# mLSTM stage: value and output-gate tiles between the heads' steps, values turned by identity products, fewer one-row products

## The chip, the core and the metric

The kernel runs on one core of a Trainium2 chip. The metric is the device time of one execution in microseconds (us); lower is better. TensorE (PE) multiplies, ScalarE (ACT) and VectorE (DVE) work on tiles, SyncE (SP) issues the DMAs that stream the weights.

## The reference

Two blocks of two layers each over x of 512 tokens x 1024 channels, all in float32. The first block is attention with convolution and Fourier branches and gates, for a context of 256 tokens and for x. The second has a convolution/LRU mixer in layer 0 and an mLSTM mixer in layer 1, each followed by a gated feed-forward part. What the change touches:

```
# first block, each layer and stream: the value heads of attention
z = h @ w_in[l];  v = z[..., OFF_V:OFF_G]            # 128 channels: 2 heads x 64
o = einsum('bgrqk,bkgd->bqgrd', softmax(q k^T / 8), v)

# second block, layer 1: mLSTM, 8 heads, q and k 64 wide, v and o 128 wide
u = xn @ w_in + b_in;  q, k, v, o, ig, fg = split(u)
# per head, causal over the sequence, b = cumsum(log_sigmoid(fg))
d_w    = exp(b_j - b_s + ig_s - m_j)
scores = (q k^T / 8) * d_w
h      = scores @ v / max(|sum(scores)|, exp(-m))
h      = h * rsqrt(mean(h*h) + 1e-6) * head_g
h      = sigmoid(o) * h
out    = h @ w_out
```

## The kernel before

**Layout.** Activations lie with channels on partitions and the 512 tokens along the free dimension. A matrix is streamed as tiles of 128 x 1024 numbers (512 KB) through a ring of four buffers. `split` on ACT rounds a tile to `w_hi` (L680), `lower_w` on DVE makes the rest, `w_lo` (L1919); both run three tiles ahead of PE. A float32 product is three PE products, `three` (L1251 to L1253): hi x hi, lo x hi and hi x lo. One tile of 128 output channels is 8 blocks x 3 = 24 products of 512 columns (`product`). An ordinary tile is read by ACT and then `posted` by DVE; PE's `ready` waits for both `w_ready` and `post`.

**Order.** Each engine runs one hand-written program in order; semaphores join them. There is no scheduler.

**mLSTM stage before.** After the norm `pre_mix`, `ml_qk` works 8 q/k tiles and 8 output-gate tiles with sigmoid, `ml_gates` one tile of the input and forget gates, `ml_v` 8 tiles of values in two halves. `ml_v` wants tokens on partitions, so there the activations are the loaded operand and the weights stream, and the bias row is added by one-row products (L1732), two per token block. Then `mlstm` runs head by head. A head has four steps n (128 keys each). `spread` copies the head's two rows over all partitions by two products of 8 rows (L1757, float32). `score_t` (L1772, L1773) makes the transposed scores of a step, DVE adds the causal mask (`diagonal`, L2565), ACT takes exponentials (L871, L873), DVE multiplies (`weights`, L2575), ACT and DVE split the result (`upper_part` L883, `lower_part` L2582), PE multiplies by the values and by ones (`values`, L1251 to L1253 and L1788, L1789). `query_key_parts` of the next head (L865 on ACT, L2554 and L2555 on DVE) stands in step 1. After a head, DVE makes the denominator (L2592, L2593), ACT copies and squares the numerator (L889, L890) and squares the denominator (L897), PE sums the squares in `total` (L1797, and one-row products L1798). At the end `small` gets the roots, PE spreads them (L1828) and DVE does three operations per head (L2619, L2624, L2627), the second of which multiplies by the output gate. No weight tile is worked in `mlstm`.

**Attention before.** At the end of the tiles of a block, `v_tile` on PE makes the values with tokens on partitions: per token block of 128, 8 x 3 products of only 128 columns. `attention` mixes the heads' steps with other weight tiles (`fill`); ACT and DVE split a tile (`split`, `lower_w`) at its last block, k == 7. At its end DVE does `reciprocals(1)` (L2204) and then raises `post` (L2249), for which the next stage `merge` waits on PE.

## Time and profile before

| | us |
|---|---|
| median of 3 runs (3703.87 to 3711.55) | 3707.84 |
| the profiled execution, whole | 3709.84 |
| its span | 3708.1 |
| PE busy in it | 3425.5 (92%) |
| DVE busy | 2104.3 (57%) |
| ACT busy | 1268.1 (34%) |
| mean granted TensorE clock, share of full speed | 0.927 |

The profile holds one execution. "Busy" of PE is modelled from the starts of pipelined products, so a busy PE can still be at half its clock; the granted clock is a column of its own. A wait is put down to the operation that released it.

### The profile page before, as it was taken

Reading aid. Unit: us, or ns where it says so; the run is one execution under the profiler, and the core shown is the slowest. Engines: PE = TensorE matmul, PEld = TensorE weight load, DVE = VectorE, ACT = ScalarE, POOL = GpSimd, SP = SyncE. Lnnn points to the kernel's source line nnn. Section 1 sums busy time; section 2 is a strip of 40 time slices with the busy share of each in tenths; the row PEclk is TensorE's granted clock in tenths of the full one; section 3 lists DMA queues with packets and bytes.
Section 4 is the critical chain, followed back from the end, with each engine's and each line's share of the span. In section 5 each row is a group of like instructions: output and inputs, shape, how many; then the busy total and the mean of one; then the engine's idle time right before and its main releaser. Section 6 shows DMA issues by size and latency. Waiting matters only on the chain.

```text
span 3708.1 us, 45259 instructions
## 1 busy us (share of the span) xinstructions
PE 3425.5 (92%) x16528; PEld 2802.7 (76%) x16528; DVE 2104.3 (57%) x2898; ACT 1268.1 (34%) x1816; POOL 0.2 (0%) x4
## 2 busy tenths in 40 slices
PE   6999999998999999998999999469999898889997
PEld 4888988776778877876878887257888765678886
DVE  7767876664565555655565557764335323453335
ACT  5554443554222223354222223222222324432221
POOL 0000000000000000000000000000000000000000
PEclk8999999999999999999999999679999895589998
DMA  6554542323222222222222222112223220013221
GB/s 216 188 190 148 184 143 86 119 97 102 85 91 96 96 88 89 79 80 80 91 85 96 96 96 68 34 46 84 98 97 103 68 74 6 1 53 101 96 97 68
DMA packets 98583, 353.69 MB, mean 95 GB/s; under 512 B 10641, under 2 KB 11793, under 8 KB 98450
## 3 DMA queue, kind: packets, MB, share of 16 engines
q1 hardware_dynamic: 98160, 350.82, 28.5%
q8 instruction: 89, 1.46, 0.2%
q10 hardware_dynamic: 290, 1.05, 0.1%
q14 instruction: 44, 0.36, 0.0%
HBM read 349.73 MB, written 2.10 MB: 95 GB/s over the span
## 4 chain that ended last, share of the span: by engine, by line
PE 84%; DVE 10%; ACT 3%; issue 1%; DMA 1%; DVEq 0%; ACTq 0%; SPq 0%
PE ring L1251 23%; PE ring L1252 22%; PE ring L1253 22%; PE ring L1500 2%; PE bank L1251 2%; PE bank L1253 2%; PE bank L1252 2%; PE bank L1292 2%; DVE z L2398 1%; DVE w_lo L1919 1%; ACT w_hi L680 1%; DVE scr L1962 1%; DVE h_lo L1968 1%; PE bank L1757 1%; PE ring L1529 1%
## 5 line engine op out<-in xcount | busy, mean ns | idle before, releaser
L1251 PE MATMUL ring<-h_hi,w_hi 128*128 128x512 f32 (+1 forms) x2888 | 1088.6, 377 | 58.8 <-DVE h_lo L1968 30.4
L1919 DVE TENSOR_TENSOR w_lo<-raw,w_hi 128x1024 fp32r<-128x1024 f32 x658 | 803.6, 1225 | 521.8 <-ACT w_hi L680 499.6
L1252 PE MATMUL ring<-h_lo,w_hi 128*128 128x512 f32 (+1 forms) x2888 | 1073.2, 372 | 0.0
L1253 PE MATMUL ring<-h_hi,w_lo 128*128 128x512 f32 (+1 forms) x2888 | 1072.0, 371 | 0.0
L680 ACT ACTIVATE w_hi<-raw 128x1024 fp32r<-128x1024 f32 x658 | 693.1, 1056 | 812.4 <-PE ring L1253 728.1
L1251 PEld LDWEIGHTS ring<-h_hi,w_hi 128*128 128x128 f32 x2888 | 554.5, 192 | 182.4 <-issue 55.6
L1253 PEld LDWEIGHTS ring<-h_hi,w_lo 128*128 128x128 f32 x2888 | 555.6, 192 | 92.3
L1252 PEld LDWEIGHTS ring<-h_lo,w_hi 128*128 128x128 f32 x2888 | 557.0, 193 | 84.4
L1251 PE MATMUL ring<-y_hi,w_hi 128*128 128x512 f32 (+1 forms) x1328 | 488.7, 368 | 33.7 <-DVE y_lo L1935 26.2
L1252 PE MATMUL ring<-y_lo,w_hi 128*128 128x512 f32 (+1 forms) x1328 | 485.7, 366 | 0.0
L1253 PE MATMUL ring<-y_hi,w_lo 128*128 128x512 f32 (+1 forms) x1328 | 485.4, 366 | 0.0
L1251 PEld LDWEIGHTS ring<-y_hi,w_hi 128*128 128x128 f32 x1328 | 251.0, 189 | 82.3 <-DVE y_lo L1935 28.8
L1253 PEld LDWEIGHTS ring<-y_hi,w_lo 128*128 128x128 f32 x1328 | 251.2, 189 | 40.4
L1252 PEld LDWEIGHTS ring<-y_lo,w_hi 128*128 128x128 f32 x1328 | 251.3, 189 | 39.2
L1183 ACT ACTIVATE scr<-ring 128x512 f32<-128x512 f32 (+1 forms) x96 | 50.6, 527 | 295.2 <-PE ring L1253 295.2
L2303 DVE SCALAR_TENSOR_TENSOR x<-ring,mod,x 128x512 f32<-128x512 f32 (+1 forms) x80 | 60.0, 751 | 155.5 <-PE ring L1253 155.5
L2324 DVE TENSOR_TENSOR z<-scr 128x512 f32<-128x512 f32 (+1 forms) x96 | 57.9, 603 | 153.3 <-ACT scr L1183 153.3
L2200 DVE TENSOR_TENSOR y_lo<-z,y_hi 128x512 fp32r<-128x512 f32 (+1 forms) x112 | 72.4, 648 | 74.5 <-ACT y_hi L1103 74.0
L2190 DVE TENSOR_REDUCE mx<-ring 128x1 f32<-128x768 f32 (+1 forms) x80 | 67.9, 849 | 69.8 <-PE ring L1530 69.2
L1103 ACT ACTIVATE y_hi<-bank 128x512 fp32r<-128x512 f32 (+1 forms) x112 | 63.6, 568 | 106.7 <-PE bank L1253 106.3
L1979 DVE TENSOR_TENSOR scr<-scr 128x512 f32<-128x512 f32 (+1 forms) x152 | 93.8, 617 | 5.2
L2506 DVE TENSOR_TENSOR z<-z,ring 128x512 f32<-128x512 f32 x48 | 33.0, 688 | 110.8 <-PE ring L1253 110.8
(286 smaller groups left out, 3340.2 us busy)
## 6 DMA issues: line engine op xcount, KB each, us to landing
raw<-ws SPq DMA_DIRECT2D x658, 512.0 KB, 3.3
x<-x_t SPq DMA_DIRECT2D x1, 2048.0 KB, 14.6
out_t<-x SPq DMA_DIRECT2D x1, 2048.0 KB, 7.3
xc<-ctx_t SPq DMA_DIRECT2D x1, 1024.0 KB, 9.7
z<-ropes ACTq DMA_DIRECT2D x2, 512.0 KB, 3.5
mat<-mats SPq DMA_DIRECT2D x1, 320.0 KB, 4.4
vec<-vecs SPq DMA_DIRECT2D x1, 216.5 KB, 2.6
xc<-bv ACTq DMA_DIRECT2D x1, 4.0 KB
```

What stands on the lines that cost most here:

```text
L680: nc.scalar.activation(w_hi[:, t % R, :], raw[:, t % R, :], ACT.Copy).then_inc(w_hi_ready, 1)
L1103: nc.scalar.activation(y_hi[:, 4 + k % 2, :T], bank[k % 2][:, :T], ACT.Exp, scale=HEAD ** -0.5)\
L1251: nc.tensor.matmul(o, a_hi, b_hi, start=start, stop=False)
L1252: nc.tensor.matmul(o, a_hi, b_lo, start=False, stop=False)
L1253: return nc.tensor.matmul(o, a_lo, b_hi, start=False, stop=stop)
L1292: m = nc.tensor.matmul(bank[tt][:, 0:1], src[:, tt * P:(tt + 1) * P], ones[:, 0:1], start=k == 0, stop=is_summed or k == KB - 1)
L1500: m = nc.tensor.matmul(fl.bank(job)[0:4, 0:256], c_parts[:, n % 2 * 4 + k // 2, :], weights, start=(n % 2, k) == (0, 0), stop=(n % 2, k) = ...
L1919: nc.vector.tensor_tensor(w_lo[:, u, :], raw[:, u, :], f(w_hi[:, u, :]), ALU.subtract).then_inc(w_ready, 1)
L1979: step(nc.vector.tensor_tensor(total, total, scr[:, 3, :T], ALU.add))
L2190: nc.vector.reduce_max(mx[:, h % 2, qt:qt + 1], view[:, 0:n_kt * P], AX_X).then_inc(s_max, 1)
L2200: nc.vector.tensor_tensor(y_lo[:, b, :T], src, f(y_hi[:, b, :T]), ALU.subtract).then_inc(s_p, 1)
L2303: step(nc.vector.scalar_tensor_tensor(o, ring[:, c % R, :T], g, o, ALU.mult, ALU.add), post)
```

## The change

In the mLSTM stage the gate tile comes first, then 9 tiles (8 of q/k and the values of head 0). The other 7 value tiles and the 8 output-gate tiles become `fill` inside `mlstm`: 16 block products a head, 6, 2, 4 and 4 of them in steps 0 to 3 (head 7: one tile). A value tile is now made with channels on partitions, gets its bias by ACT, and is turned to tokens on partitions by four float32 products with the identity (`v_turned`). The bias comes by 8 new loads on SP at the kernel's start instead of one on ACT. Output gates are Tanh with a half of the bias instead of Sigmoid, and DVE multiplies the numerator by 1 + tanh when it takes it from PSUM; the factor two goes into the root (scale 4/P). The denominator's square is added on DVE into one row of the squares, so `total` has 4 products where it had 8. The row spread for the denominator and the products by ones have 32 output rows instead of 128. In the first block `v_tile` becomes an ordinary tile and `v_turned`, `split` and `lower_w` of a fill tile stand at its first block, and `post` is raised ahead of the last reciprocal.

```diff
@@ plan, mLSTM @@
-    add("ml_qk", 16)
     add("ml_gates", 1)
-    add("ml_v", 8)
-    add("mlstm", 0)
+    add("ml_qk", 9)
+    add("mlstm", 15)
@@ SP @@
+            for h in range(N_HEADS):
+                sp.dma_start(v_bias[:, h:h + 1], bv_in[0:1, h * P:(h + 1) * P].rearrange("o p -> p o")).then_inc(s_bv, 16)
@@ ACT, mlstm @@
+                def v_upper(h):
+                    act.wait_ge(s_turned, C.next(s_turned))
+                    nc.scalar.activation(v_parts(y_hi, h), turned_bank(h).rearrange("p (t d) -> p t d", d=P), ACT.Copy)\
+                        .then_inc(hi_ready, 1)
+                def fill(h, n):
+                    if h == 7 and n > 1:
+                        return
+                    t = 2 * h + n // 2
+                    c = first + t
+                    if n % 2 == 0:
+                        split(c)
+                        return
+                    done(c)
+                    if t % 2 or h == 7:
+                        nc.scalar.activation(z[:, 8 + h, :], fill_bank(h, 1), ACT.Tanh, bias=o_bias[:, h:h + 1],
+                                             scale=0.5).then_inc(s_gate_read, 1)
+                    else:
+                        nc.scalar.activation(z[:, 15, :], fill_bank(h, 0), ACT.Identity, bias=v_bias[:, h + 1:h + 2])\
+                            .then_inc(s_gate_read, 1)
+                    if n == 3:
+                        v_upper(h + 1)
@@ PE, mlstm @@
+                def v_turned(h):
+                    if h:
+                        pe.wait_ge(s_gate_read, gate0 + 2 * h - 1)
+                    for tt in range(4):
+                        s = slice(tt * P, (tt + 1) * P)
+                        m = nc.tensor.matmul(turned_bank(h)[:, s], z[:, 15, s], ident, start=True, stop=True)
+                    m.then_inc(s_turned, 1)
-                    nc.tensor.matmul(ring[:, 3, j], ones_r[:, :], kv[:, b, j], start=n == 0, stop=False)
+                    nc.tensor.matmul(bank[3][0:32, j], ones_r[:, 0:32], kv[:, b, j], start=n == 0, stop=False)
-                        nc.tensor.matmul(o, xv[:, h % 2, t], ones[:, 0:1], start=True, stop=False)
-                        m = nc.tensor.matmul(o, den_sq_row[:, t], ones[HEAD:HEAD + 1, 0:1], start=False, stop=True)
+                        m = nc.tensor.matmul(bank[1][:, 4 * h + tt:4 * h + tt + 1],
+                                             xv[:, h % 2, tt * P:(tt + 1) * P], ones[:, 0:1], start=True, stop=True)
                     for n in range(4):
                         if n < 2:
                             score_t(h, n + 2)
-                        elif h + 1 < N_HEADS:
+                        elif more:
                             score_t(h + 1, n - 2)
+                        if more:
+                            fill(h, (range(6), range(6, 8), range(8, 12), range(12, 16))[n])
+                        elif n < 2:
+                            fill(h, (range(6), range(6, 8))[n])
                         if n == 1 and h:
                             total(h - 1)
+                        if n == 3 and more:
+                            v_turned(h + 1)
                         values(h, n)
@@ DVE, mlstm @@
+                    dve.wait_ge(s_gate_read, gate0 + (2 * h + 2 if h < 7 else 15))
+                    issue(nc.vector.scalar_tensor_tensor(head_out(h), z[:, 8 + h, :], 1.0, ring[:, 2, :],
+                                                         ALU.add, ALU.mult), s_gated)
+                def denominator(h):
+                    step(nc.vector.scalar_tensor_tensor(den_row, den_row, float(P * EPS), den_row, ALU.mult, ALU.mult))
+                    sq = xv[one_row, h % 2, :]
+                    issue(nc.vector.tensor_tensor(sq, sq, den_row, ALU.add), s_den_sq)
-                        issue(nc.vector.tensor_tensor(o, o, z[:, 8 + n - 1, :], ALU.mult), t_ready)
@@ attention, PE @@
-                        m = three(bank[3][:, s], h_hi[:, k, s], h_lo[:, k, s], *w(c, k), k == 0, k == KB - 1)
+                    m = nc.tensor.matmul(bank[3][:, s], z[:, 13, s], ident, start=True, stop=True)
@@ attention, ACT; DVE's lower_w(c) alike @@
+                        if k == 0:
+                            split(c)
                         if k < 7:
                             continue
-                        split(c)
@@ attention, DVE, its end @@
-                reciprocals(1)
                 dve.sem_inc(post, len(fl.tiles))
                 C.next(post, len(fl.tiles))
+                reciprocals(1)
```

PE, step 0 of head 1 in `mlstm`, before, from its values on: L1251 to L1253 are the values' three products, L1788 and L1789 those by ones, L1757 the spread of head 2, L1772 and L1773 the last scores, L1797 and L1798 the total of head 0.

```order
L1251 MATMUL ring<-kv,y_hi 128x512
L1252 MATMUL ring<-kv,y_hi 128x512
L1253 MATMUL ring<-kv,y_lo 128x512
L1788 MATMUL ring<-kv,ones_r 128x512
L1789 MATMUL ring<-kv,ones_r 128x512
L1757 MATMUL bank<-xc,mat 128x512 x2
L1772 MATMUL ring<-kv 128x128
L1773 MATMUL ring<-kv 128x128
L1797 MATMUL bank<-mat,xc 128x1
L1798 MATMUL bank<-mat,xc 128x1
```

The same place now; L1279 to L1281 are the three products, with `h_hi` and `w_hi` those of a fill tile, and `32x512` has 32 output rows.

```order
L1833 MATMUL bank<-kv,ones_r 32x512
L1834 MATMUL bank<-kv,ones_r 32x512
L1799 MATMUL bank<-xc,mat 128x512
L1801 MATMUL bank<-xc,mat 32x512
L1814 MATMUL ring<-kv 128x128
L1815 MATMUL ring<-kv 128x128
L1279 MATMUL bank<-h_hi,w_hi 128x512
L1280 MATMUL bank<-h_lo,w_hi 128x512
L1281 MATMUL bank<-h_hi,w_lo 128x512
```

Two block products of a fill tile (six rows) now stand between the last scores and the total; six blocks, four and four stand in the other steps.

DVE, steps 0 and 1 of a head, before: weights, denominator of the head before (two rows L2592, L2593), diagonal, lower part, then step 1 and the query and key parts of the next head (L2554, L2555).

```order
L2575 TENSOR_TENSOR scr<-ring,scr 128x384
L2592 TENSOR_TENSOR xc<-ring,xc 1x512
L2593 SCALAR_TENSOR_TENSOR xc<-ring,xc 1x512
L2565 TENSOR_TENSOR scr<-xc,mat 128x128
L2582 TENSOR_TENSOR kv<-scr,kv 128x512
L2575 TENSOR_TENSOR scr<-ring,scr 128x256
L2565 TENSOR_TENSOR scr<-xc,mat 128x128
L2582 TENSOR_TENSOR kv<-scr,kv 128x384
L2554 TENSOR_TENSOR kv<-z,kv 64x512
```

Now, from the lower half of the turned values (L2641) on:

```order
L2641 TENSOR_TENSOR y_lo<-ring,y_hi 128x4x128
L2613 TENSOR_TENSOR scr<-ring,scr 128x384
L2627 TENSOR_TENSOR xc<-bank,xc 1x512
L2628 SCALAR_TENSOR_TENSOR xc<-bank,xc 1x512
L2631 SCALAR_TENSOR_TENSOR z<-z,ring 128x512
L2603 TENSOR_TENSOR scr<-xc,mat 128x128
L2620 TENSOR_TENSOR kv<-scr,kv 128x512
L2635 SCALAR_TENSOR_TENSOR xc<-xc 1x512
L2637 TENSOR_TENSOR xc<-xc 1x512
L1967 TENSOR_TENSOR w_lo<-raw,w_hi 128x1024
L2613 TENSOR_TENSOR scr<-ring,scr 128x256
L2603 TENSOR_TENSOR scr<-xc,mat 128x128
```

Ahead of the diagonal of step 2 (L2603) stands the gated numerator (L2631), and ahead of that of step 3 also two row operations and a whole `w_lo`.

DVE, the end of the attention of x in layer 0, before and after; L2204 and L2252 are the same reciprocal, L2178 and L2226 the columns of the modulation:

```order
L2169 TENSOR_TENSOR z<-z,scr 128x512
L1919 TENSOR_TENSOR w_lo<-raw,w_hi 128x1024
L2178 TENSOR_TENSOR mod<-ring,vec 128x4
L2204 RECIPROCAL scr<-scr 128x512
L1919 TENSOR_TENSOR w_lo<-raw,w_hi 128x1024 x2
```

```order
L2219 TENSOR_TENSOR z<-z,scr 128x512
L2226 TENSOR_TENSOR mod<-ring,vec 128x4
L2252 RECIPROCAL scr<-scr 128x512
L1967 TENSOR_TENSOR w_lo<-raw,w_hi 128x1024 x2
L2310 TENSOR_TENSOR z<-z,bank 128x512 x2
```

The last `w_lo` has gone from between the last tile's sum and the reciprocal to ahead of it; the raise of `post`, no row of its own, stood behind the reciprocal and stands ahead of it.

## Rows read from the trace of the kernel before

**Rows 1.** Busy time by stretch: start:end, length, busy us (instructions) PE PEld DVE ACT POOL, granted clock, DMA.
```profile
2800.00:2850.00 50.00, 50.00 (x222) 41.38 (x222) 21.08 (x26) 12.56 (x14) 0.00 (x0) 1.00 0.31 104
...
3100.00:3150.00 50.00, 46.68 (x127) 32.59 (x126) 17.20 (x38) 21.20 (x45) 0.00 (x0) 0.50 0.00 0
```

**Rows 2.** Chain that ended last, in the mLSTM stage: start us, length us, engine and line.
```profile
2998.38 1.05 PE bank L1732 x2
...
3069.77 3.79 PE bank L1757 x4
...
3078.62 0.77 PE ring L1251
...
3097.18 3.70 PE bank L1757 x4
...
3117.36 3.70 PE bank L1757 x4
...
3225.40 0.71 DVE xc L2592
...
3232.05 3.45 PE bank L1828 x16
3235.52 0.75 DVE z L2619
```

**Rows 3.** Instructions grouped by line, 2900 to 3250: busy us, mean ns, idle before.
```profile
L1797 PE MATMUL bank<-mat,xc 128*128 128x1 f32 x64 | 18.6, 359 | 2.3 <-ACT xc L897 2.3
```

**Rows 4.** Instructions in order of time in one head's steps 0 and 1: start, length, engine.
```profile
3112.44 0.70 DVE L2592 TENSOR_TENSOR xc<-ring,xc 1x512 f32<-1x512 f32 x1 [0.64 <-PE ring L1789]
...
3114.22 0.40 ACT L871 ACTIVATE scr<-scr,small 128x128 f32<-128x128 f32 x1 [0.18 <-DVE scr L2565]
...
3117.01 2.58 ACT L865 ACTIVATE kv<-z 64x512 fp32r<-64x512 f32 x4
```

**Rows 5.** PE alone, stretches of 5 us in `ml_v`: busy (instructions), granted clock, DMA share, GB/s.
```profile
3000.00:3005.00 5.00, 5.00 (x17) 1.00 0.00 0
...
3035.00:3040.00 5.00, 5.00 (x9) 0.50 0.00 0
```

**Rows 6.** PE alone, stretches of 2 us in and behind an attention.
```profile
798.00:800.00 2.00, 2.00 (x9) 0.50 0.61 211
...
892.00:894.00 2.00, 1.89 (x5) 0.50 0.00 0
...
896.00:898.00 2.00, 2.00 (x8) 0.79 0.08 31
```

**Rows 7.** PE's waits, context (52:290) and x of layer 0 (540:900): us, times, longest.
```profile
PE ring L1251 <- DVEq L2249: 3.2, 1, 3.2
...
PE ring L1500 <- ACT z L1066: 5.9, 6, 2.4
PE ring L1251 <- DVEq L2249: 5.0, 1, 5.0
```

**Rows 8.** DVE in order of time, end of the attention of x, layer 0.
```profile
887.23 1.23 DVE L1919 TENSOR_TENSOR w_lo<-raw,w_hi 128x1024 fp32r<-128x1024 f32 x1
...
888.56 3.35 DVE L2204 RECIPROCAL scr<-scr 128x512 f32<-128x512 f32 x1
```

**Rows 9.** PE in order of time: first and last of `v_tile`'s 48; then float32 128x128; total-like sums.
```profile
111.75 0.22 PE L1251 MATMUL bank<-w_hi,h_hi 128*128 128x128 f32 x1
...
116.95 0.28 PE L1253 MATMUL bank<-w_hi,h_lo 128*128 128x128 f32 x1
...
101.96 0.45 PE bank L1375 x4
...
2875.48 1.05 PE L1292 MATMUL bank<-mat,scr 128*128 128x1 f32 x8 [2.29 <-DVEq L1982]
```

**Rows 10.** The start: chain of waits; then the DMA queue's packets, MB, share in 8:20.
```profile
7.69 12.23 DMA raw<-ws
...
q1 hardware_dynamic: 2493, 4.65, 104.8%
```

More of the change, by code:

```diff
@@ L969, in v_tile, with v_upper @@
                 done(c)
+                nc.scalar.activation(z[:, 13, :T], bank[2][:, :T], ACT.Copy).then_inc(evac, 1)
+            def v_upper(stream):
+                T = length(stream)
+                act.wait_ge(s_turned, C.next(s_turned))
                 kt = 0 if stream == "main" else SEQ // P
@@ L1569, in attention @@
                     fill(qt)
-                pe.wait_ge(post, first + R)
+                    if qt == 0:
+                        if main:
+                            pe.wait_ge(s_rot_read, C.next(s_rot_read, 5))
+                        v_turned(stream, first + R)
                 max_row(0)
@@ new lines, in fill @@
+                def fill(h, steps):
+                    for s in steps:
+                        t, k = 2 * h + s // 8, s % 8
+                        c, gate = first + t, t % 2 or h == 7
+                        if k == 0:
+                            pe.wait_ge(w_ready, c + 1)
+                            if h == 7:
+                                pe.wait_ge(s_gate_read, gate0 + 14)
+                            elif gate:
+                                pe.wait_ge(s_fill_read, fill0 + h + 1)
+                            elif h:
+                                pe.wait_ge(s_gate_read, gate0 + 2 * h)
+                        m = three(fill_bank(h, t % 2), *w(c, k), h_hi[:, k, :], h_lo[:, k, :], k == 0, k == 7)
+                        if k == 7:
+                            m.then_inc(tile_done, 1)
@@ L1742, in mlstm @@
+                v_turned(0)
                 pe.wait_ge(s_row, C.next(s_row, 2))
@@ L2604, in mlstm @@
                     if n == 0 and h:
-                        denominator(h - 1)
+                        numerator(h - 1)
                     if k + 2 < 4 * N_HEADS:
```

278 lines of the change are left out of this document (135 added, 143 removed).

## Prediction

> **What bounds the kernel now.** I read the busy times by stretch first, then the chain of waits, then single instructions. In a stretch of plain tiles PE is busy all the time at full clock: 222 products of 512 columns in 50 us [rows 1], 0.225 us each, so a tile of 24 costs 5.40 us. In the mLSTM stage PE is again 93% busy, but at a granted clock of 0.50 (1.2 GHz), and no weights are streamed [rows 1]. So the stage is bound by PE at half its clock, and for a smaller part by the handing on between PE, ACT and DVE. One head takes 20.2 us, from one spread to the next (3097.18 to 3117.36) [rows 2]. Two things can be won: a pass of work less, and the clock.
>
> A difference of 0.2% (7 us) is about what a measurement of this kernel can tell from none. All sums stand against the profiled execution, 3709.8 us with a span of 3708.1; the median of the runs is 2 us lower, which I take into the range.
>
> **The mLSTM stage, on PE.** The old stage from the first bias product to the end of the last values runs from 2998.4 to 3225.4 [rows 2]. Seven of the 16 tiles ahead of it have moved into the heads, so the new stage starts 7 x 5.40 = 37.8 us earlier, at 2960.6; old length from there 264.8 us.
>
> New prices at full clock. 512 columns 0.225, 384 in proportion 0.169, 256 about 0.115 and 128 columns 0.111 (48 products from 111.75 to 116.95 [rows 9]): a set of a head's four widths is 0.62 us. A head has two sets for the scores and five for the values and ones, 4.3 us. Fewer output rows change none of this, since the columns stay. The spread is two float32 products: 3.70 us at half clock [rows 2]; at full clock between 1.85 (half) and 2.1 (the one-row product of the same width, 1.05 each [rows 2]); I take 1.95. The total has four products, 8 instructions: 1.05 us [rows 9] where 16 cost some 4.1 at half clock (64 instructions of L1797 begin the same way [rows 3]). Turning the values is four float32 products, 8 instructions at the 0.112 of four in 0.45 [rows 9], 0.9 us. With two tiles, 10.8, a head is 19.0 us on PE. Over the stage: 15 tiles 81.0, scores and values 8 x 4.33 less the two scores ahead of it 34.2, seven times spread, total and turn 27.3; together 142.5 us.
>
> To this come, in order:
> - Start. From the last tile's end to the third score there are ACT's copy, the turn, the columns, the spread, ACT's and DVE's parts of q and k, exponentials and weights. From the spread to the first values the old kernel took 8.9 us (3069.77 to 3078.62 [rows 2]). With 1.0 for copy and post, 0.9 for the turn, 1.3 for the columns, and the last 1.4 of the old chain now under fill, less 2 for a spread at full clock: 8.7 us. PE is half idle there, so 1 us for a start at half clock.
> - The wait for query and key parts. I walk a head from the end of the last values. DVE does the lower half of the turned values, weights, the two row operations (0.71 each [rows 4]) and the gated numerator by 3.4 us and the diagonal by 3.7; ACT's exponentials end at 4.4, its threshold row at 5.0, the split of a tile at 6.1; DVE's `w_lo` (1.23 [rows 8]) at 7.3, weights and diagonal of step 3 at 8.0; ACT's exponential (0.40 [rows 4]) at 8.4, its four parts (2.58 [rows 4]) at 10.9, DVE's two of 0.7 at 12.3. PE reaches the first scores of the next head at 10.7: 4.3 to the values of step 0, then 1.1, 1.95, 0.1, 1.35 of fill, 1.05 and 0.8. It waits 1.6 us. Bounds 0 and 3; seven heads, 11.2 us. At step 0 the same walk has lower part and PE meet at 4.3, no wait. The last head has half a fill: 1.5 us.
> - The clock. Full clock held through alternating one-row and dense products (1.00 at 3000) but, once low, stayed low under the same mix (0.50 at 3035) [rows 5]. Ten dense block products a head will raise it. But spread, total and the wait of 1.6 us stand close together, and in the attention short waits dropped it for some 3 us (0.50 at 798 [rows 6]). I count one such drop in most heads: 1.2 us for each of eight, 10 us. Bounds 0 and 31 (below).
> Sum 8.7 + 1 + 142.5 + 11.2 + 1.5 + 10 = 174.9, against 264.8: **89.9 us gained**.
>
> ACT and DVE carry more, but hide. By the busy times a head of 20.2 us holds 8.6 us of ACT and 6.9 of DVE [rows 1]. ACT gets two splits, two readings and the turned copy and loses two operations; were each of the five as long as `w_lo` (1.23 [rows 8]), it would come to 15. DVE gets two `w_lo`, four operations of 0.7, 12 in all. Both lie under 21 of PE. If that cover goes, the wait above is where it shows.
>
> The end. Before, 23.9 us from the last denominator (3225.40) to `mix_out`; the final loop from 3235.52 [rows 2] had three operations a head on DVE. One goes: 8 x 0.6 less the part that overlaps, 3.8 us. DVE has three more operations ahead of the last total where ACT had one, +1.4; eight instructions fewer in it, -1.5. **3.9 us gained**.
>
> **The value tiles of the first block.** x: 96 products of 128 columns at 0.111 are 10.6 us [rows 9]; now 5.40 and a turn of 0.9, 4.3 gained, twice. Context: 5.3 becomes 2.9 + 0.45, 2.0 gained, twice. PE is the bound there. **12.6 us**, bounds 8 and 13.
>
> **The raise of `post`.** PE waits 5.0 us at `merge` in x of layer 0, and for the same line and as long in layer 1; 3.2 in the context [rows 7]. In those waits lie `w_lo` 1.23, then the reciprocal of 3.35 [rows 8]. Both leave them: `w_lo` to the tile's start, the reciprocal behind `post`. Left is the small column operation, 0.4 us a time, so 12.0 gained. Late next is the reciprocal itself, which PE wants only behind the second tile, over 5 us later. The clock falls to 0.50 behind such a wait and stays low into the stretch at 896 [rows 6]: 5 us at half clock cost 2.2 us of work there, and where it rises sooner 1 or less; 3.7 in all. **15.7 us**, bounds 12 and 16.
>
> **`split` at the tile's start.** PE waits for the reading of a gate 5.9 us in six places in x of layer 0 [rows 7], since ACT does the split (about 1 us, under DVE's 1.23) ahead of it. Up to 1 us a place can go, about as much in layer 1, and some in the context; but the split now stands ahead of exponentials. **6 us gained**, bounds -3 (a loss) and 14.
>
> **The start.** SP issues 8 loads of 128 single numbers behind x and ahead of the first streamed tile, and the chain runs through that tile: 12.23 us of waiting for its DMA, then ACT and DVE [rows 10]. No row shows packets of 4 bytes. 2493 packets, mostly of 1 to 2 KB, took 12 us, 4.8 ns each [rows 10]; the 1024 new ones would take 4.9 us if each costs the same. Bounds 0 (queue not full) and 8. I take a **loss of 5 us**. The Trainium skill, "DMA: Bandwidth & Descriptors", section "Latency and other measured facts", speaks against this edit: a non-contiguous last dimension lowers to one descriptor per element, which is the count of 1024 above. By that page's table a 4 KB load of 64 packets takes 0.68 us, an estimate of 10.9 us for 1024 at the same rate; the sum would be 6 us worse. No row here decides it.
>
> **Sum.** 89.9 + 3.9 + 12.6 + 15.7 + 6 - 5 = 123.1; 3709.8 - 123.1 = 3586.7. **Forecast 3587 us.**
>
> **Rivals.**
> - Full clock and full cover: no drop, and parts in time. For it: the clock held at 3000 [rows 5], and in the attention most short waits didn't drop it. Against: my walk. 10 + 11 less: 3566.
> - Two drops a head, one behind spread and total, one at the wait, each as long as at the start of `merge` (892 into 896 [rows 6], 2.2 us lost): 7 x 2 x 2.2 = 31 instead of 10: 3608. For it: the half clock of the old stage through the same spread [rows 1]. The Trainium skill, "TensorE: Matmul & The Clock Gate", Part 4, says that transposes in PE's transpose mode don't count as busy for the clock; these are plain products with an identity, and it would make this rival likelier if it held for them. The four identity products in 0.45 us [rows 9] ran at full clock.
> - Slower: the fill hides nothing. If PE did the 15 tiles between chains that last as before, at half clock (15 x 10.8 = 162 us beside the old 155.6), the stage would be 8.7 + 318 - 14 for products saved, 312 against 264.8: 47 lost, 4 gained at the end, 29 elsewhere: 3724. It decides where a head takes over 36 us. Against it: six blocks of dense products a head, and at the start of `merge` such a stretch raised the clock within 5 us [rows 6].
> - The edits of attention don't pay, since other engines are late next, and the start costs 8: some 15 worse, 3602; it is inside the range.
>
> **How the numbers follow.** Forecast 0.53 with its sizes (3572 to 3602), full clock and cover 0.2, two drops 0.22, slower 0.02, something that eats all of the gain 0.03. The range 3558 to 3618 takes in the second and third with the bounds of the small terms. Faster 0.96, same 0.02, slower 0.02.
>
> **What would show it.** Granted clock in the heads: mean of 0.85 to 0.95, low for 2 to 4 us at the query and key parts. A head of 21 to 22 us. PE's waits there on DVE's `kv` of the parts, 1 to 2 us. `merge` without its 5.0. The first streamed tile landing at 25 instead of 19.95. The forecast is wrong by most if the clock is 0.5 through whole heads, or if PE waits in several steps of a head.

## The result and the profile after

The changed kernel takes 3573.0 us (median of 4 runs, 3571.23 to 3575.05); the kernel before, timed beside it, 3706.8 (3703.87 to 3711.55). The ratio is 0.9638 with a 95% interval of 0.9627 to 0.965: 134 us or 3.6% faster. The forecast was 3587, the range 3558 to 3618. The profiled execution takes 3571.2 us whole, with a span of 3569.4 (before: 3709.8 and 3708.1), so 138.6 us less where the sum of the forecast had 123.1. The mean granted clock rose from 0.927 to 0.951.

To see where the time went, I read one mark in each stage from the chain of waits: the start of the products that spread the reciprocal root (L1299 before, L1327 after). The stages between the marks:

| stage, between marks | before | after | gained | forecast |
|---|---|---|---|---|
| start | 59.38 | 60.79 | -1.4 | -5 |
| context block | 266.19 | 264.57 | 1.6 | 5.8 |
| x, layer 0 | 495.15 | 479.58 | 15.6 | |
| context's pass in layer 1 | 20.61 | 17.62 | 3.0 | |
| x, layer 1 | 475.11 | 458.29 | 16.8 | 28.5 for these three |
| mLSTM (2897.71 to 3295.90; 2862.65 to 3158.39) | 398.19 | 295.74 | 102.4 | 93.8 |

All other stages agree within 0.7 us. The forecast column is the sum's terms split by place.

**The heads.** Busy time by stretch, the view of [rows 1], of the changed kernel: start:end, length, busy us (instructions) of PE, PEld, DVE, ACT, POOL, then granted clock and DMA.

```profile
2950.00:3000.00 50.00, 48.43 (x244) 37.17 (x243) 26.90 (x51) 28.19 (x54) 0.00 (x0) 1.00 0.16 53
3000.00:3050.00 50.00, 49.13 (x218) 35.65 (x216) 29.70 (x56) 27.16 (x52) 0.00 (x0) 0.93 0.12 43
```

Before, a stretch like this had 127 products at a clock of 0.50; now it has 244 at 1.00, PE is as busy, and ACT and DVE, which had 21 and 17 us of work in 50, have 28 and 27. The chain of waits, the view of [rows 2] (start, length, engine and line):

```profile
2926.11 1.16 PE ring L1764 x8
...
2943.07 1.05 PE bank L1799 x2
2944.11 0.97 PE bank L1801 x2
...
2963.30 1.05 PE bank L1799 x2
...
2967.11 0.79 PE bank L1841 x8
...
2968.89 0.71 issue
2969.59 0.47 PE ring L1814
...
2976.70 0.89 PE ring L1764 x8
...
2983.72 1.05 PE bank L1799 x2
...
3094.16 0.69 DVE xc L2627
...
3100.17 3.56 PE bank L1880 x16
```

L1799 and L1801 are a head's spread, 2.02 us where the old one took 3.70. L1841 is the total, 0.79 us; L1764 the turn of the values, 0.89. From spread to spread a head takes 20.2 us (2943.07 to 2963.30) and 20.4 (to 2983.72): as long as before, but with 16 block products more in it. The others take 20.7, 22.7, 20.7 and 20.5. The "issue" of 0.71 us ahead of the first scores (L1814) is PE's wait for DVE's query and key parts. The waits of PE from 2915 to 3115 (us, times, longest):

```profile
PE ring L1814 <- issue: 4.0, 5, 0.9
PE bank L1841 <- DVE xc L2637: 3.5, 1, 3.5
PE ring L1814 <- DVE kv L2593: 1.6, 1, 1.6
```

The second is the last total, behind five operations of DVE (four on a row and the gated numerator). The third stands ahead of the scores of head 0, so it belongs to the start of the stage. And PE alone in the one long head, the view of [rows 5]:

```profile
3007.50:3010.00 2.50, 2.50 (x13) 0.55 0.42 167
3010.00:3012.50 2.50, 2.50 (x9) 0.50 0.00 0
3012.50:3015.00 2.50, 2.50 (x8) 0.58 0.00 0
3015.00:3017.50 2.50, 2.50 (x15) 1.00 0.58 210
```

The clock falls to its lower level 3 us behind that head's spread (3004.31) while PE is busy all the time, and is back 7 us later. That is 2.2 us of a head. In the first of the six intervals there is a shorter one, of 3.4 us (2945 to 2950); in the other four the clock is at 1.00. The shorter one isn't free either: in e_post and e_lower (below) it is missing, and this interval takes 18.65 us instead of 20.2.

**The attention.** PE's waits in x of layer 0 from 520 to 900, which answer to [rows 7]:

```profile
PE ring L1531 <- ACT z L1094: 2.7, 6, 1.3
...
PE ring L1279 <- DVEq L2298: 0.5, 1, 0.5
```

The wait of 5.0 us for `post` is 0.5, and the clock stays at 1.00 behind it, where [rows 6] had 0.50. PE's waits in the context block, 60 to 325 (before, the same lines had 2.6 us in three places for z and 1.7 for `y_lo`):

```profile
PE ring L1279 <- DVE z L2216: 7.5, 5, 2.8
PE ring L1560 <- DVE y_lo L2190: 3.8, 1, 3.8
```

**The start.** Chain of waits, as in [rows 10]:

```profile
6.80 3.78 SPq L670
15.46 5.84 DMA raw<-ws
```

L670 is the loop of the eight bias loads; they hold SP's queue for 8.3 us, the first alone for 3.8. The first streamed tile is issued at 15.46 instead of 7.69, but takes 5.84 us instead of 12.23, and lands at 21.3 instead of 19.9. From 8 to 22 us the DMA engines were full in both kernels (packets take 105% and 106% of their time). The DMA view from 8 to 22, before and after:

```profile
DMA packets 2726, 5.48 MB, mean 391 GB/s; under 512 B 109, under 2 KB 1133, under 8 KB 2726
DMA packets 3748, 5.02 MB, mean 358 GB/s; under 512 B 1244, under 2 KB 2268, under 8 KB 3748
```

In the same 14 us there are some 1020 packets more and 0.46 MB less. At 391 GB/s that is 1.2 us, an estimate from these two lines of what the single numbers cost, and nearly the 1.4 us of the mark.

### The profile page after: what moved, and what is told of

Its sections match the earlier page's. It is cut to its first block, busy times and chain, and to the rows that moved or that the text cites. A ratio compares the mean times of both kernels' runs of the same rounds, so it can differ in the third digit from the quotient of the medians.

```text
span 3569.4 us, 44839 instructions
## 1 busy us (share of the span) xinstructions
PE 3314.2 (93%) x16344; PEld 2725.1 (76%) x16344; DVE 2112.5 (59%) x2919; ACT 1261.0 (35%) x1808; POOL 0.2 (0%) x4
## 3 DMA queue, kind: packets, MB, share of 16 engines
q10 hardware_dynamic: 288, 1.05, 0.1%
## 4 chain that ended last, share of the span: by engine, by line
PE 84%; DVE 10%; ACT 3%; issue 2%; DMA 1%; SPq 0%; DVEq 0%; ACTq 0%
PE ring L1279 23%; PE ring L1281 23%; PE ring L1280 23%; PE ring L1531 2%; PE bank L1279 2%; PE bank L1320 2%; PE bank L1280 2%; PE bank L1281 2%; DVE w_lo L1967 1%; DVE z L2448 1%; DVE scr L2010 1%; DVE h_lo L2016 1%; ACT w_hi L698 1%; PE ring L1560 1%; PE ring L1561 1%
## 5 line engine op out<-in xcount | busy, mean ns | idle before, releaser
L1279 PE MATMUL ring<-h_hi,w_hi 128*128 128x512 f32 (+1 forms) x2896 | 1086.2, 375 | 42.0 <-DVE h_lo L2016 31.0
L1281 PE MATMUL ring<-h_hi,w_lo 128*128 128x512 f32 (+1 forms) x2896 | 1070.5, 370 | 0.0
L1279 PEld LDWEIGHTS ring<-h_hi,w_hi 128*128 128x128 f32 x2896 | 552.2, 191 | 163.6 <-issue 40.6
L1281 PEld LDWEIGHTS ring<-h_hi,w_lo 128*128 128x128 f32 x2896 | 553.6, 191 | 91.8
L1279 PE MATMUL ring<-y_hi,w_hi 128*128 128x512 f32 (+1 forms) x1328 | 488.6, 368 | 39.4 <-DVE y_lo L1983 26.2
L1281 PE MATMUL ring<-y_hi,w_lo 128*128 128x512 f32 (+1 forms) x1328 | 485.9, 366 | 0.0
L1279 PEld LDWEIGHTS ring<-y_hi,w_hi 128*128 128x128 f32 x1328 | 251.6, 189 | 86.7 <-DVE y_lo L1983 28.8
L1281 PEld LDWEIGHTS ring<-y_hi,w_lo 128*128 128x128 f32 x1328 | 251.7, 189 | 40.2
L1213 ACT ACTIVATE scr<-ring 128x512 f32<-128x512 f32 (+1 forms) x96 | 50.6, 527 | 295.2 <-PE ring L1281 295.2
L2027 DVE TENSOR_TENSOR scr<-scr 128x512 f32<-128x512 f32 (+1 forms) x152 | 93.8, 617 | 5.2
L2549 DVE TENSOR_TENSOR z<-ring,scr 128x512 f32<-128x512 f32 x44 | 30.4, 691 | 107.9 <-PE ring L1281 107.9
```

Of the source, the lines that this page charges most:

```text
L1279: nc.tensor.matmul(o, a_hi, b_hi, start=start, stop=False)
L1281: return nc.tensor.matmul(o, a_lo, b_hi, start=False, stop=stop)
L2027: step(nc.vector.tensor_tensor(total, total, scr[:, 3, :T], ALU.add))
```

## The experiments

Every version is the changed kernel with the edit shown. "Common" below is a stage's mean over the seven profiles in which the first block's code is that of the changed kernel; in these, the context block takes 266.2 us (264.6 to 267.2), x of layer 0 478.3 (477.6 to 479.6), x of layer 1 458.8 (458.3 to 459.2) and the context's pass 17.1 (16.7 to 17.6). By this the context block gained nothing against the 266.2 of before. The mLSTM stage, in six profiles with its code unchanged, takes 292.3 to 297.8, mean 295.2: it varies by the dips of the clock.

### Undoing the edits of the attention

**e_post**, the reciprocal ahead of the raise again:

```diff
-                dve.sem_inc(post, len(fl.tiles))
-                C.next(post, len(fl.tiles))
                 reciprocals(1)
+                dve.sem_inc(post, len(fl.tiles))
+                C.next(post, len(fl.tiles))
```

> The changed kernel with one edit undone: the last reciprocal of the attention (3.35 us on DVE) stands again ahead of the raise of post. My theory, the term of the forecast: merge waits for it again, 3.0 to 4.5 us in each of the two x layers and about 3 us in the context, and in x the granted clock falls behind the wait for another 1 to 2 us. The sum is 10 to 16 us slower than the 3573.0 us of the changed kernel, so 3583 to 3589; the stages of x layer 0 and of x layer 1 each 5 to 7 us longer, the context block 2.5 to 3.5. Rival: PE would wait there for another engine in any case (the column operation, ACT), and less than 5 us comes back in all.

Measured: 3586.4 us (3584.7 to 3587.7), 13.4 slower than 3573.0. PE's waits from 860 to 920, and PE alone behind them:

```profile
PE ring L1279 <- DVEq L2299: 4.9, 1, 4.9
```

```profile
885.00:890.00 5.00, 1.00 (x3) 0.65 0.00 0
890.00:895.00 5.00, 5.00 (x17) 0.67 0.35 105
```

The wait is back, and behind it the clock, with 17 products where a stretch at full clock has some 24. The rival falls. By stage: context 4.5 longer than common (I expected 2.5 to 3.5), x 5.8 and 5.6.

**e_split**, split and lower part of a fill tile again at its last step:

```diff
@@ ACT, attention fill @@
-                        if k == 0:
-                            split(c)
                         if k < 7:
                             continue
+                        split(c)
@@ DVE, attention fill @@
-                        if k == 0:
-                            lower_w(c)
...
-                        if k == 7 and t in fl.columns:
-                            columns(*fl.columns[t])
+                        if k == 7:
+                            lower_w(c)
+                            if t in fl.columns:
+                                columns(*fl.columns[t])
```

> The changed kernel with one edit undone: in the attention's fill the split of a tile on ACT and its lower part on DVE stand again at the tile's last step. Theory of the forecast: 6 us slower (3579), 2 to 3 us in each x layer with PE's waits for the reading of a gate back from 2.7 to near 5.9 us in x of layer 0, and about 1 in the context. Rival, from the changed kernel's trace: in the context the lower part now stands ahead of DVE's branch sums, and PE's waits for these sums (z) went from 2.6 to 7.5 us; then undoing it makes the context block 2 to 4 us shorter than now (264.6 us between its first and last marks), while x gets 5 to 8 us longer in both layers together; time 3574 to 3578.

Measured: 3579.5 us (3574.1 to 3583.9), 6.4 slower, the size of the forecast's term. But it is a sum of two signs, as the rival had it, and both are larger than the rival had them: x longer by 6.7 and 5.2 us (5 to 8 together expected), the context block shorter by 5.4 (2 to 4). The four runs spread over 10 us, so the stages tell more here than the whole time. PE's waits for gate readings in x (520 to 900) are the old ones of [rows 7]:

```profile
PE ring L1530 <- ACT z L1093: 5.9, 6, 2.4
...
PE ring L1278 <- DVEq L2297: 1.6, 1, 1.6
```

**e_lower**, only the DVE half of that diff; ACT's split stays at the first step.

> The changed kernel with only DVE's lower part of a tile back at the tile's last step in the attention's fill; ACT's split stays at the first step. If the gain of this edit lies in ACT's order alone, x keeps all of it except the lower part's 1.23 us in the last wait of each layer (1 us each), and if DVE's order is what costs in the context, the context block is 2 to 4 us shorter than now: time 3569 to 3573. If DVE's order has nothing to do with the context's poor gain, the context stays within 1 us of 264.6 us and the sum is 2 to 4 us slower: 3575 to 3577.

Measured: **3561.9 us** (3559.9 to 3566.0), 11 faster than the changed kernel and 7 below the lower end of what I expected; ratio to before 0.9605, interval 0.9589 to 0.9621, which doesn't touch that of the changed kernel. The context block is 4.9 us shorter than common, x of layer 0 0.5 and of layer 1 2.1, 7.5 in the stages that it touches; the rest lies in the start and the mLSTM stage, which vary by as much with their code unchanged. So all of this edit's gain is ACT's (e_split to this version: 17.6 us, 14 by stages), and DVE's half is a loss. PE's waits in the context block of this version:

```profile
PE ring L1279 <- DVE z L2214: 2.6, 3, 1.3
PE ring L1560 <- DVE y_lo L2190: 2.5, 1, 2.5
```

The 7.5 us are 2.6 again. What happened is seen on DVE of the changed kernel, in order of time (start, length, line):

```profile
145.16 3.81 DVE L1967 TENSOR_TENSOR w_lo<-raw,w_hi 128x1024 fp32r<-128x1024 f32 x3 [0.74 <-ACT w_hi L698]
148.88 0.41 DVE L2216 SCALAR_TENSOR_TENSOR z<-z,ring 128x256 f32<-128x256 f32 x1
...
248.67 1.22 DVE L1967 TENSOR_TENSOR w_lo<-raw,w_hi 128x1024 fp32r<-128x1024 f32 x1 [1.23 <-ACT w_hi L698]
249.81 0.41 DVE L2216 SCALAR_TENSOR_TENSOR z<-z,ring 128x256 f32<-128x256 f32 x1
```

L2216 is a branch sum that frees a bank PE waits for: at 250.28 PE starts after 2.80 us of idleness that end with it. Three lower parts stand ahead of one sum, or DVE stands 1.23 us in the wait for ACT's split with the sum queued behind it. That the lower parts can come later at no cost is what e_lower shows.

**e_value**, the value tiles of the first block as before, 128 columns a product (PE's part shown; ACT and DVE go back to one reading and one lower part):

```diff
+                for tt in range(T // P):
+                    s = slice(tt * P, (tt + 1) * P)
+                    for k in range(KB):
+                        m = three(bank[3][:, s], h_hi[:, k, s], h_lo[:, k, s], *w(c, k), k == 0, k == KB - 1)
-                product(c + 8, T, h_hi, h_lo, o=bank[2][:, :T])
-                        v_turned(stream, first + R)
```

> The changed kernel with one edit undone: the value tiles of the first block and of the context's pass in layer 1 are again computed with tokens as rows, 128 columns a product, without the identity products. Theory of the forecast: 4.3 us slower in each x layer and 2.0 in the context block and in the context's pass, 12.6 in all, 3585.6. Rival, from the changed kernel's trace: in the context block PE reaches the first scores and waits there 3.8 us for the query's lower part (1.7 before), so most of its 2.0 us never came and nothing goes away there: 10 us or less, 3581 to 3583, with the context block within 0.7 us of 264.6 us.

Measured: 3591.0 us (3588.3 to 3593.7), 18 slower, so more than the forecast's 12.6 and more than the rival. By stage 5.1 and 4.7 in x, 3.5 in the context's pass and 0.9 in the context block: 14.2 in all, of which the forecast had 12.6. The rest is in the start (0.5) and in the mLSTM stage (297.8, the top of what that unchanged stage takes), so not of this edit. As the rival said, the context block gives nearly nothing: PE comes to the first scores earlier and waits there (3.5 us in this version, 3.8 in the changed kernel).

The undone edits add up. In x of layer 0, 5.8 + 6.7 + 5.1 = 17.6 against 16.9 between before and common; layer 1, 5.6 + 5.2 + 4.7 = 15.5 against 16.3; context, 4.5 - 5.4 + 0.9 = 0.0 against 0.0.

### What holds the heads at 20 us

**e_thin** and **e_half**: of each tile in the heads only blocks 0 and 7, or 0, 2, 4 and 7.

```diff
+                        if k not in (0, 7):
+                            continue
                         m = three(fill_bank(h, t % 2), *w(c, k), h_hi[:, k, :], h_lo[:, k, :], k == 0, k == 7)
```

> The changed kernel without six of the eight blocks of each of the 15 tiles that are worked in the heads of the mLSTM stage (blocks 1 to 6 are left out, so value and gate tiles aren't whole); all waits, splits and the streaming of weights stay. 90 blocks at 0.675 us are 60.8 us of PE's work at full clock, 8.1 in a whole head of 20.2 to 20.7 us. Theory: the dense blocks are what holds the clock up in the heads; without them it falls back to 0.50 as in the kernel before, where the rest (19.0 - 8.1 = 10.9 us at full clock) takes near 20 us again: a head of 17 to 21 us, the whole within 25 us of 3573 (3548 to 3580). Rival 1: the clock is high for another reason (fewer one-row products, shorter waits), then a head is bound by ACT's 15 us or less: 12 to 15 us a head, 3525 to 3535 or below, with a granted clock over 0.9.

> The changed kernel with four of the eight blocks of each of the 15 tiles in the heads (blocks 1, 3, 5 and 6 are left out, so value and gate tiles aren't whole): 60 blocks or 40.5 us of work at full clock less, 5.4 in a head. With two of eight the heads took 20.8 to 21.5 us at a clock of 0.64. Theory: what the blocks don't do, the clock takes back: a head of 18.5 to 21 us at a clock between 0.7 and 0.9, 3560 to 3573. Rival: half the blocks are enough to hold the clock, then a head is bound by PE's 13.6 us or ACT's 15: 15 to 16 us, 3535 to 3545.

Measured: e_thin 3570.9 us (3567.1 to 3573.6), e_half 3571.9 (3571.7 to 3572.1). Leaving out 60.8 us of PE's work gains 2 us, and leaving out 40.5 gains 1. The same two stretches of the changed kernel, of e_half and of e_thin:

```profile
2975.00:3000.00 25.00, 24.14 (x125) 18.57 (x124) 12.85 (x25) 14.49 (x27) 0.00 (x0) 1.00 0.16 56
3025.00:3050.00 25.00, 24.13 (x112) 16.45 (x110) 15.65 (x30) 15.07 (x29) 0.00 (x0) 1.00 0.13 43
```

```profile
2975.00:3000.00 25.00, 21.59 (x88) 15.01 (x86) 15.37 (x29) 13.97 (x27) 0.00 (x0) 0.80 0.13 43
3025.00:3050.00 25.00, 23.00 (x81) 15.37 (x80) 13.78 (x26) 14.96 (x29) 0.00 (x0) 0.72 0.20 63
```

```profile
2975.00:3000.00 25.00, 19.28 (x64) 12.56 (x65) 15.62 (x30) 14.54 (x28) 0.00 (x0) 0.67 0.13 43
3025.00:3050.00 25.00, 21.64 (x74) 15.08 (x73) 13.59 (x25) 13.13 (x25) 0.00 (x0) 0.64 0.13 43
```

With fewer dense blocks the clock falls: over five heads, 2959 to 3066, it is 0.97 in the changed kernel, 0.74 in e_half and 0.66 in e_thin. From the second interval on a head takes 20.8 to 22.3 us (e_half) and 20.8 to 21.5 (e_thin), no less than 20.5; only the first is shorter (17.1 and 18.6). So most of the blocks is paid by the clock that they hold up. It isn't the clock alone: in e_thin PE also waits 24.6 us in eight places (3.5 at the longest) for `lower_part`, DVE's lower half of the multiplied scores, behind a chain of some 11 us through ACT and DVE (2987.24 to 2998.16). An estimate from these numbers: a head of e_thin has 19.0 - 8.1 = 10.9 us of work at full clock, which at 0.66 is 16.5, and 3.5 of waiting makes 20.0, near the 20.8 to 21.5 measured. So of the 8.1 us left out, the clock takes back 5.6, and the waits cost the rest and more. How short such a head would be at full clock no run shows, since the waits could change with it.

**e_clump**: all 16 blocks in step 0.

```diff
-                            fill(h, (range(6), range(6, 8), range(8, 12), range(12, 16))[n])
+                            fill(h, (range(16), (), (), ())[n])
```

> The changed kernel with all 16 blocks of a head's two tiles in the head's first step instead of 6, 2, 4 and 4 in its four steps. The same products in the same number. Theory: spread over the steps the blocks stand beside ACT's and DVE's work for each step; in one lump they cover only the first, and the other three steps wait for the handing on between DVE, ACT and PE, 1 to 1.5 us each, and the clock falls behind such waits: a head of 22.5 to 25 us instead of 20.2 to 20.7, 3588 to 3605. Rival: ACT and DVE have 15 and 12 us of work in a head and PE 19, so any order is near PE's bound, and the clock is held by the amount of dense work alone: 20 to 21.5 us, 3570 to 3580.

Measured: 3585.1 us (3583.1 to 3586.6), 12 slower, 22.0 to 22.8 us a head: the same work in one lump costs 1.5 us a head, less than my theory had, in the direction it had. Waits from 2915 to 3090:

```profile
PE ring L1279 <- DVE kv L2620: 5.1, 7, 1.7
```

That is seven times some 0.7 us. The clock over these heads is 0.86 to 0.93 in five stretches of 25 us and 1.00 in the sixth. So both the cover and the clock depend on where the blocks stand.

**e_total**: the total's products twice.

```diff
-                    for tt in range(4):
+                    for tt in (0, 1, 2, 3, 0, 1, 2, 3):
```

> The changed kernel with the four products of a head's total issued twice (the second time they write the same values), so 16 instructions of one column instead of 8, as many as in the kernel before. Price of the removed one-row products. Theory of the forecast: 1.05 us for 8 instructions (0.8 to 0.95 measured after), so 6 to 8 us for eight heads, 3579 to 3581, the clock as now. Rival 1: they also make the clock fall in most heads, 2.2 us each, 15 more: 3590 to 3596. Rival 2: PE waits behind them for the values of step 1 anyway: within 2 us of 3573.

Measured: 3575.9 us (3575.4 to 3576.4), 2.9 slower, between the theory and the second rival. Five of its six intervals are 20.2 to 20.6 us, as without the doubling, and the wait of 0.7 to 0.9 us at the next scores (L1814 <- issue) is gone from the list of waits: the doubled products fill it. One takes 25.2, with the clock low 3 us behind its spread; chain of waits, and PE alone:

```profile
2962.59 1.05 PE bank L1799 x2
...
2967.18 3.20 PE bank L1841 x16
```

```profile
2965.00:2967.50 2.50, 2.50 (x10) 0.58 0.63 210
2967.50:2970.00 2.50, 2.50 (x13) 0.50 0.00 0
```

So the eight one-row products a head that the change removed cost little in this order of work. They would be worth 0.8 us a head only where no wait follows.

### The wait for the query and key parts, and the dips

**e_shift**: two blocks of step 2 ahead of the next head's first scores.

```diff
                         elif more:
+                            if n == 2:
+                                fill(h, range(8, 10))
                             score_t(h + 1, n - 2)
...
-                            fill(h, (range(6), range(6, 8), range(8, 12), range(12, 16))[n])
+                            fill(h, (range(6), range(6, 8), range(10, 12), range(12, 16))[n])
```

> The changed kernel with two of the four blocks of step 2 moved ahead of the first scores of the next head, where PE waits 0.7 to 0.9 us in each of seven heads for DVE's query and key parts. The two blocks take 1.35 us. Theory: that wait is on the path and nothing else is late next: 0.7 to 0.8 us a head less, 5 to 6 us in all, 3567 to 3568. Rival: the values of step 2 need DVE's weights and lower part, which are queued behind the same query and key parts, so PE waits there instead: within 2 us of 3573.

Measured: 3570.8 us (3566.3 to 3572.8), 2.2 faster, so not the 5 of the theory; by the whole time alone it can hardly be told from none, and the intervals of the heads decide. The wait between heads is gone and no other takes its place: heads take 19.5 us, 1.0 less than 20.5. But two of the six intervals are 22.7, and the first is 20.2. PE alone in one of these (its spread starts at 2964.5):

```profile
2967.50:2970.00 2.50, 2.50 (x10) 0.50 0.44 169
2970.00:2972.50 2.50, 2.50 (x10) 0.50 0.00 0
2972.50:2975.00 2.50, 2.50 (x8) 0.65 0.00 0
```

There is no wait in the whole head. In four other profiles the dip stands at the same distance behind a spread (e_bias 2959.7 and 2962.5, e_lower 3034.8 and 3037.5, e_total, and the changed kernel). It is not in every profile: in e_post, with the same code in the heads, the clock is at 1.00 through all six intervals (PE alone, from the second spread to the last):

```profile
2959.80:3081.10 121.30, 117.45 (x569) 1.00 0.15 50
```

**e_behind**: e_best (below) with two of the six blocks of step 0 moved behind the spread.

```diff
-                            fill(h, (range(6), range(6, 8), range(10, 12), range(12, 16))[n])
+                            fill(h, (range(4), range(4, 8), range(10, 12), range(12, 16))[n])
```

> The version with the three edits together, and in the mLSTM stage two of the six fill blocks of step 0 moved behind the spread, into step 1 (4, 4, 4, 4 instead of 6, 2, 4, 4). The granted clock fell in one or two of seven heads, each time about 3 us behind a spread, also where PE waited for nothing. Theory: the thin stretch of spread, scores, two blocks and total is what lets it fall; with four blocks behind the spread it holds in all heads, 2.2 us less for each dip that goes, unless the values of step 0 now wait for the gated numerator (up to 1 us a head, 7 us in all): 0 to 5 us faster or slower than the version without it, with a mean clock of 1.00 from the second head on. Rival: the dips have nothing to do with the fill behind the spread: the same one or two dips.

Measured: 3573.7 us (3571.6 to 3579.2), 11 slower than e_best, outside what I expected. Three heads take 24.0 us and a fourth 22.5. PE waits for the values of step 0:

```profile
PE ring L1279 <- DVE kv L2622: 7.9, 6, 1.3
```

1.3 us a head, right ahead of the spread, and the clock of these heads falls to 0.84 and 0.85 over 25 us; in the three it falls within 1 us of the spread's start. It tells what covers what: the six blocks of step 0 hide the row operations, the gated numerator and the lower part. Four blocks behind the spread didn't prevent the dips, but there was now a wait ahead of it, so the run doesn't tell what they would do without the wait. What decides in which head the clock dips stays open.

### The start, and all together

**e_bias**: one load of the bias, issued by ACT.

```diff
-            for h in range(N_HEADS):
-                sp.dma_start(v_bias[:, h:h + 1], bv_in[0:1, h * P:(h + 1) * P].rearrange("o p -> p o")).then_inc(s_bv, 16)
...
             def ml_qk(first):
+                act.dma_start(v_bias[:, :], bv_in.rearrange("o (h p) -> p (o h)", p=P), allow_slow_non_contiguous=True)\
+                    .then_inc(s_bv, 16)
```

> The changed kernel with the bias of the values loaded by one DMA of the same 1024 single numbers, issued by ACT at the start of the query and key tiles, instead of eight issued by SP behind x. Theory: SP's eight issues (8.3 us of its queue) hold up the first streamed tile, whose split starts at 21.32 us instead of 19.95: 1.4 us faster, the first mark at 59.4 instead of 60.8. The forecast's term would have been 5 us. Rival: the single numbers slow whatever is loaded beside them, wherever they are issued: then the same 1 to 5 us show up at the query and key tiles. In the whole time little to be seen: 3570 to 3574.

Measured: 3570.6 us (3569.7 to 3573.6), 2.5 faster, which by the whole time alone can't be told from none. The first mark stands at 58.5; in the ten profiles with eight loads on SP it stands at 59.9 to 62.8, mean 61.7; in the three with one load on ACT at 58.5, 58.8 and 61.3. The DMA issues of this version and of the changed kernel (KB each, median us from issue to landing):

```profile
v_bias<-bv ACTq DMA_DIRECT2D x1, 4.0 KB, 2.2
```

```profile
v_bias<-bv SPq DMA_DIRECT2D x8, 0.5 KB, 7.4
```

So the single numbers are cheap where nothing is queued with them. At the kernel's start they cost because their packets stand ahead of the first streamed tile at DMA engines that are full (the two lines under "The start"), and not, as my theory had it, because SP issues the tile later: before, that tile was issued 7.8 us sooner and waited. By the marks the cost can be told only roughly, 1 to 3 us.

**e_best**: e_lower, e_shift and e_bias together.

> The changed kernel with the three edits together: DVE's lower part back at the last step in the attention's fill, two fill blocks moved ahead of the next head's first scores in the mLSTM stage, the value bias as one load issued by ACT. Apart they gave -11, -2 and -2.5 us against 3573.0. Theory: they lie in different stages and add up: 3555 to 3560. Rival: what the early start saves is lost again, or two more dips of the clock in the heads take what the filled wait gives: 3560 to 3564, no better than the first of them alone (3561.9).

Measured: 3562.6 us (3559.2 to 3564.9, 5 runs), ratio 0.9602, interval 0.9589 to 0.9615. It is 10 us faster than the changed kernel, but not better than e_lower alone (3561.9): the rival held. Its mLSTM stage takes 292.3 us, with two heads of 21.1 and 22.7 between heads of 19.5.

## Why the forecast came out as it did

**The stage as a whole: right, and sized too carefully.** From the first turn (2926.11) to the last head's row operations (3094.16) are 168.1 us, where I had 174.9. The start of the stage is right: 2926.11 plus the 35.1 us gained in the stages ahead of it is 2961.2, the forecast said 2960.6. PE's prices held too: spread 2.02 (1.95), turn 0.89 (0.9), total 0.79 to 0.95 (1.05). One part of the gain has no experiment of its own: in the kernel before, the eight value tiles took 71.4 us from the first bias product to the first spread, with PE like this:

```profile
2998.40:3069.80 71.40, 63.41 (x217) 0.87 0.18 62
```

Eight tiles at 5.40 are 43.2, so some of the stage's gain comes from the value tiles leaving `ml_v` with its one-row products and its half clock, wherever they had gone; how much no run separates.

**Wrong size, the wait for query and key parts.** I had 1.6 us in seven heads, 11.2; it is 0.7 to 0.9, 4.0 us in five heads (in the profile's list). My walk put DVE at 12.3 and PE at 10.7. In the head whose last values end at 2977.8, DVE's parts are done 12.3 us later, as I had it, and PE comes to the scores after 11.5: PE was 0.8 off, which is half of the difference. e_shift shows the wait on the path: filled, a head is 1.0 us shorter.

**Wrong size and wrong place, the clock.** I had one drop of 1.2 us in each of eight heads, at the wait and the thin stretch together. There is one dip of 2.2 us and a short one of some 1.6 in six intervals, and in e_post there is none; in e_shift there are dips without any wait in the head. The place was half right: it is behind the spread. That dense blocks raise the clock and hold it was the step that the forecast rested on, and e_thin and e_half show it from the other side.

**Somewhat too small, the end, and from another place.** I had 3.9 gained and took 23.9 us from the last denominator (3225.40) to `mix_out`. But the first product of `mix_out` stood already at 3240.60, 15.2 us behind it, and now it stands 15.7 us behind (3094.16 to 3109.86): nothing is gained there. The gain lies inside `mix_out`, where PE had waited for the final loop (3225 to 3297, before):

```profile
PE ring L1251 <- DVE h_lo L2627: 3.0, 4, 0.9
```

With two operations a head on DVE (0.66 and 0.60) instead of three these waits are gone. From the ninth block of `mix_out` on PE is 5.4 us ahead of the old distance, and at the next mark 6.3.

**Right, `post`**: 15.7 forecast, 13.4 by e_post, with 5.8 and 5.6 in x where I had 6.5, and more in the context (4.5) than its wait of 3.2.

**Right sum, wrong reasons, the early split.** 6 us forecast, 6.4 measured, but as +12 in x and -5.4 in the context. The step that failed is "`w_lo` to the tile's start", which I took as free and even as a gain: I counted what it takes out of one wait (1.23 us) and not what is queued behind it on DVE. In the context block, 120 to 260, DVE is busy 12.8 to 15.5 of 20 us (ACT 9.6 to 14.2), and the branch sums that PE waits for stood behind. My lower bound of -3 was made for ACT, not for this. It is the largest single thing I missed: 11 us by the whole time, 7.5 by the stages.

**Value tiles: right in x (4.9 for 4.3), too little in the context's pass (3.5 for 2.0), too much in the context block (0.9 for 2.0)**, where the next wait took it.

**The start: right direction, too large.** 5 us forecast; 1.4 in the pair of profiles, some 2 to 3 by all of them. The step that failed is the price of a packet: I took 4.8 ns, that of packets of 1 to 2 KB, for packets of 4 bytes. Some 1020 packets more took the place of 1.2 us of transfer, about 1.2 ns each (an estimate from the two lines under "The start"). The Trainium skill, "DMA: Bandwidth & Descriptors", has the rule of one descriptor for each element in its section "Rules for kernel authors" and the table in its section "Bandwidth", not where I had placed them. The count agrees with the packets above; the table gave an estimate of 10.9 us, and since the one load of e_bias landed 2.2 us after its issue, the trace doesn't bear this out as a time.

**The rivals.** "Full clock and full cover" (3566) was nearest in its mechanism: the clock is at 1.00 through four of six intervals. "Two drops a head" falls; of the Trainium skill's rule on transposes ("TensorE: Matmul & The Clock Gate", Part 4) nothing is seen here: the identity products of a head (8 instructions) run in stretches with a clock of 1.00, among dense ones, and no run tells how they would count alone. "The fill hides nothing" wanted heads of over 36 us; they take 20.2 to 22.7. "Attention edits don't pay" falls for x and holds for the context block.

## What to carry to other kernels

Where a stage is a chain of small steps at a low granted clock, dense work of a neighbouring stage between its steps may be free twice, by filling waits and by holding the clock: price it by leaving the work out, and spread it by what each step has to cover. When a step is moved earlier, ask on each engine apart what is queued behind it: the same move gained some 14 us on ACT, which had more room, and lost 7.5 to 11 on DVE, where sums that PE waits for stood behind it. Undo each edit by itself also when the whole is faster, since 134 us of gain hid this loss.

## What was new of the hardware

- The granted clock dips to 0.50 for some 7 us, about 3 us behind a pair of float32 products of 8 rows (the spread), with PE busy all the time, and in none (e_post), one or two (e_shift) of six like heads. A dip costs 2.2 us, in e_total, where it is longer, 4.7.
- The mean clock of a head falls by degrees with the dense blocks in it (0.97, 0.74 and 0.66 with 8, 4 and 2 of 8 blocks of a tile), since the clock changes between its two levels within a head; the time of a head hardly follows.
- Eight small loads occupy the issuing queue for 8.3 us, the first alone for 3.8. Their 1024 single numbers took the place of 1.2 us of transfer at full DMA engines (an estimate), and one load of the same numbers, issued when little else is queued, lands after 2.2 us.
